# A four-layer model on one Trainium2 core: another order of heads, convolution inputs and taps, the sub-norm in four steps, and residual sums one chunk ahead

## The chip, the cores and the metric

The kernel runs on one core of a Trainium2 chip as one program. The metric is the device time of one execution in microseconds, taken from the hardware profiler. Five engines run their own instruction lists side by side and meet through semaphores: PE (matrix products), DVE (vector operations), ACT (activations), POOL (general work) and SP (which only issues the transfers of weights here). A wait at the head of an engine's list holds everything behind it.

## The reference, cut to what matters

512 tokens of width 1024 go through four layers and a last norm, in float32. Two of them end in a feed-forward network with a 3-tap convolution (up 1024 to 6144, gelu times value, down), the other two in one with a squared relu (width 4096).

```
# first_block: layer 0 attention, layer 1 a gated linear recurrence, each + conv_ffn
h = h + hybrid_attention_mixer(rms_norm(h), ...)   # 8 dilated heads, 4 differential heads:
    attn = p[:, :, 0] - lam * p[:, :, 1]
    ob   = rms_norm(attn @ vf, b_sub_norm) * (1 - lam_init)     # the "sub-norm"
h = h + recurrent_mixer(rms_norm(h), ...)          # uses softplus(-a_param)
# second_block: two hybrid layers
h  = rms_norm_2(x, g_mix);  split(h @ w_in) -> a_q a_k a_v b_qlat b_kvlat b_krope c_q c_k c_v c_f d_val d_gate
out_a = chunk_band_attention(a_q, a_k, a_v, rel_bias)
q  = rms_norm_2(b_qlat) @ w_uq ; kv = rms_norm_2(b_kvlat) @ w_ukv ; rotary on 32 of 96
out_b = block_causal_attention(q, k, v)            # latent heads
out_c = block_causal_attention(c_q, c_k, c_v, 1, cumsum(log_sigmoid(c_f)))   # forget heads
u = d_val * sigmoid(d_gate); u = conv31(u)         # 256 channels, 31 taps
out_d = silu(layer_norm(u))
x = x + sum_n(sigmoid(h @ w_gate + b_gate)[n] * (branches[n] @ w_branch[n])) @ w_o
x = x + square(relu(rms_norm_2(x) @ w_up)) @ w_down
```

## The kernel before, in words

The stream x is held transposed, as eight chunks of 128 channels by 512 tokens (`hT`). For exactness every product is three: operands are split into a high and a low part, and PE does high·high, high·low and low·high (L420, L421, L422 in `linear`; the same triple in L468 to L470, L541 to L543 and L770 to L772). One k-step is such a triple. The weights come as 470 slabs of 128 by 1024: SP loads one, ACT makes its high part (`w_hi`, L872), POOL the low part (`w_lo`, L1859). Three slabs are kept, so ACT's copy of slab n waits until PE has finished slab n-3.

The outputs of an activation layer are split in the same way: `take_high` (ACT, L923) and `take_low` (DVE, L1282), in that order; the pair is what PE reads next. `chunk` does it for the norm that begins a layer: ACT scales and squares a chunk (L896, L902), DVE makes its low part (L1297) and adds the squares (L1308); PE then sums over partitions and ACT and DVE make the root and its reciprocal (L917, L1323). Each product is scaled by that reciprocal on DVE afterwards (L1328). The residual sum of chunk o (L1316) adds the product's bank to `hT`.

PE writes eight banks of its accumulator memory. A bank may be written again when the reader named in `free` is done. In the hybrid layers the products go round three banks, 5, 6 and 7 (`next_bank`).

The order within a layer's attention is a list of steps written by `attention_steps`: for each block n the scores of block n, the softmax of n-1, then the extra steps that stand in `beside[n]`, then a step that is due from the sub-norm, then transposes and the mix of block n-2, then `behind[n]`. Every engine walks through the same list, each doing its part of each step. So an extra step placed early in the list stands ahead of the softmax of the next block on every engine. In the first layer the extra steps are the projections of pairs of heads (`qk`, with `qk_root`, `qk_norm`, and `qk_turn`, which transposes a pair on PE, L564), and products of the output projection (`out`, given as (output chunk, first k, last k), the sum of its parts k0 to k1 of the mixed heads y0 to y7). y4 to y7 are the differential heads with a sub-norm: `submean`, `subrec` (first half of the reciprocal, L1488), `subnorm` (second half L1491, the product L1493, and the two parts of y).

In a hybrid layer the extra steps are the latent heads' inputs (`latent`, `latent_parts`: reciprocal L1701, L1708, the split L1282), their keys, values and queries (`b_key` copied at L1720, `b_values`, `b_query`, rotated in L1663 to L1666), the forget heads' rows (`c_head`: a product of eight k-steps, and one DVE operation, L1656), the convolution's inputs (`d_input`: two products, and on DVE L1328, L1736 and L1740), 62 taps of the convolution (`tap`: even ones on DVE, L1795; odd ones a multiplication on ACT, L1225, and an addition on POOL, L1926), and the gated branches (`gated`: ten k-steps and four DVE operations). After the attention the convolution's layer norm (`conv_mean`, `conv_var`, `conv_norm`, `conv_out`) and more `gated` follow.

Of the kernel before, what the change touches and what calls it, by code (L numbers as in the profile page):

```python
# [119 lines left out]
def program(nc, x_in, small_in, fixed_in, heads_in, rel_in, pos_in, out):  # L120
# [3 lines left out]
    with ctx:  # L124
# [134 lines left out]
        def attention_steps(stage, units, beside, behind=None):  # L259
# [26 lines left out]
            for i, stage_ in enumerate(later):  # L286
                steps += beside.get(n_blocks + LAG + i, [])
                steps.append(stage_)
# [14 lines left out]
        pair_banks = [(5, 6), (7, 2)] + [((5, 6), (7, 5), (6, 7))[p % 3] for p in range(6)]  # L303
# [16 lines left out]
        parts0 = []  # L320
        for p, after in ((2, unit_steps(3)), (3, unit_steps(4)), (4, unit_steps(5)), (5, vb_steps(0))):
            parts0 += behind_next(p, after)
        parts0 += [[f] for f in unit_steps(6)] + behind_next(6, unit_steps(7))
        beside0 = {}
        for i, part in enumerate(parts0):
# [7 lines left out]
                  30: [(0, 5, 6), (1, 5, 6), (2, 5, 6)], 32: [(3, 0, 5)], 33: [(4, 0, 5)],  # L333
                  34: [(0, 6, 7), (1, 6, 7), (2, 6, 7), (3, 5, 7), (4, 5, 7)], 35: [(5, 0, 7)], 36: [(7, 0, 7)]}
# [4 lines left out]
        def qk_ready(n):  # L339
# [11 lines left out]
                   13: [("c_head", 5)], 14: [("c_head", 7)]}  # L351
# [6 lines left out]
        for i, f in enumerate(tap_list[:44]):  # L358
            behind2.setdefault(10 + i * 16 // 44, []).append(f)
# [503 lines left out]
        def scalar(A):  # L863
# [134 lines left out]
            for what, a in steps0:  # L998
# [32 lines left out]
                elif what == "subnorm":  # L1031
# [9 lines left out]


# [1080 lines left out]
```

## Time and profile before

| what | value |
|---|---|
| three runs, us | 2934.51, 2933.91, 2926.31 (median 2933.91) |
| the profiled execution, us | 2934.61, its span 2932.8, granted clock 0.982 |
| busy share | PE 96%, PE's weight loads 78%, DVE 46%, ACT 42%, POOL 42% |
| the chain that ended last | PE 85%, DVE 8%, ACT 3%, issue 2%, POOL 1% |

The profile names an instruction by its line. PE is busy nearly all the time, so what can be saved lies in PE's idle stretches, and in the stretches after them in which its clock is lower. The span is one execution; the profiled execution lies 0.7 us above the median.

### The profile page before, as it was taken

Reading aid. Unit: us, or ns where it says so; the run is one execution under the profiler, and the core shown is the slowest. Engines: PE = TensorE matmul, PEld = TensorE weight load, DVE = VectorE, ACT = ScalarE, POOL = GpSimd, SP = SyncE. Lnnn points to the kernel's source line nnn. Section 1 sums busy time; section 2 is a strip of 40 time slices with the busy share of each in tenths; the row PEclk is TensorE's granted clock in tenths of the full one; section 3 lists DMA queues with packets and bytes.
Section 4 is the critical chain, followed back from the end, with each engine's and each line's share of the span. In section 5 each row is a group of like instructions: output and inputs, shape, how many; then the busy total and the mean of one; then the engine's idle time right before and its main releaser. Section 6 shows DMA issues by size and latency. Waiting matters only on the chain.

```text
span 2932.8 us, 32425 instructions
## 1 busy us (share of the span) xinstructions
PE 2823.6 (96%) x12948; PEld 2281.5 (78%) x12948; DVE 1341.9 (46%) x2091; ACT 1223.7 (42%) x1793; POOL 1236.8 (42%) x550
## 2 busy tenths in 40 slices
PE   8998999999889999998999999999989999999998
PEld 7786788888667888876778788888767777888886
DVE  4565651545875415435656452022246565531113
ACT  3564442434544424334574434233235744342231
POOL 4222344444453444432446444444423464444442
PEclk9999999999989999998999999999999999999999
DMA  4211232232212323322222223232322222223232
GB/s 146 82 59 61 79 101 97 92 107 87 79 65 94 99 91 98 101 92 74 66 65 94 86 94 101 94 100 94 101 72 66 72 79 87 100 94 101 94 101 72
DMA packets 73926, 259.21 MB, mean 88 GB/s; under 512 B 9184, under 2 KB 9184, under 8 KB 73776
## 3 DMA queue, kind: packets, MB, share of 16 engines
q1 hardware_dynamic: 71680, 251.79, 26.8%
q10 hardware_dynamic: 2096, 5.36, 0.5%
q8 instruction: 102, 1.67, 0.2%
q14 instruction: 48, 0.39, 0.0%
HBM read 254.95 MB, written 2.13 MB: 88 GB/s over the span
## 4 chain that ended last, share of the span: by engine, by line
PE 85%; DVE 8%; ACT 3%; issue 2%; POOL 1%; DMA 0%; DVEq 0%; SPq 0%; ACTq 0%; POOLq 0%
PE ps L420 25%; PE ps L422 25%; PE ps L421 25%; PE ps L486 2%; PE ps L516 1%; PE ps L541 1%; PE ps L542 1%; PE ps L543 1%; POOL w_lo L1859 1%; PE ps L499 1%; PE ps L431 1%; PE ps L468 1%; PE ps L470 1%; PE ps L469 1%; ACT w_hi L872 1%
## 5 line engine op out<-in xcount | busy, mean ns | idle before, releaser
L1859 POOL TENSOR_TENSOR w_lo<-raw,w_hi 128x1024 fp32r<-128x1024 f32 x470 | 1135.6, 2419 | 1552.0 <-ACT w_hi L872 1551.6
L420 PE MATMUL ps<-xs,w_hi 128*128 128x512 f32 x2176 | 864.2, 397 | 17.8 <-POOL w_lo L1859 10.3
L421 PE MATMUL ps<-xs,w_hi 128*128 128x512 f32 x2176 | 849.3, 390 | 0.0
L422 PE MATMUL ps<-xs,w_lo 128*128 128x512 f32 x2176 | 849.0, 390 | 0.0
L872 ACT ACTIVATE w_hi<-raw 128x1024 fp32r<-128x1024 f32 x470 | 493.9, 1052 | 660.4 <-PE ps L422 615.4
L420 PE MATMUL ps<-hid,w_hi 128*128 128x512 f32 x1320 | 523.0, 396 | 43.7 <-DVE att L1736 18.1
L421 PE MATMUL ps<-hid,w_hi 128*128 128x512 f32 x1320 | 519.2, 393 | 0.0
L422 PE MATMUL ps<-hid,w_lo 128*128 128x512 f32 x1320 | 519.1, 393 | 0.0
L420 PEld LDWEIGHTS ps<-xs,w_hi 128*128 128x128 f32 x2176 | 409.7, 188 | 123.9 <-issue 15.0
L421 PEld LDWEIGHTS ps<-xs,w_hi 128*128 128x128 f32 x2176 | 410.0, 188 | 88.3 <-issue 4.8
L422 PEld LDWEIGHTS ps<-xs,w_lo 128*128 128x128 f32 x2176 | 409.8, 188 | 86.3
L420 PEld LDWEIGHTS ps<-hid,w_hi 128*128 128x128 f32 x1320 | 251.1, 190 | 103.9 <-DVE att L1736 19.0
L422 PEld LDWEIGHTS ps<-hid,w_lo 128*128 128x128 f32 x1320 | 251.1, 190 | 53.1
L421 PEld LDWEIGHTS ps<-hid,w_hi 128*128 128x128 f32 x1320 | 251.3, 190 | 52.0 <-issue 0.2
L1328 DVE TENSOR_TENSOR ps<-ps,rt 128x512 f32<-128x512 f32 x182 | 126.4, 697 | 267.6 <-PE ps L422 267.3
L1316 DVE TENSOR_TENSOR hT<-ps,hT 128x512 f32<-128x512 f32 x96 | 65.9, 687 | 337.7 <-PE ps L422 337.7
L1297 DVE SCALAR_TENSOR_TENSOR xs<-hT,small,xs 128x512 fp32r<-128x512 f32 x64 | 111.7, 1745 | 167.8 <-ACT xs L896 167.8
L1059 ACT ACTIVATE tmp<-ps,small 128x512 f32<-128x512 f32 x96 | 74.8, 779 | 219.4 <-DVE ps L1328 219.4
L1282 DVE TENSOR_TENSOR hid<-tmp,hid 128x512 fp32r<-128x512 f32 x120 | 85.6, 715 | 137.1 <-ACT hid L923 137.1
L930 ACT ACTIVATE pbuf<-pbuf,tiny 128x128 f32<-128x128 f32 (+3 forms) x160 | 88.7, 555 | 111.7 <-DVE tiny L1355 111.4
L1251 ACT ACTIVATE tmp<-tmp 128x512 f32<-128x512 f32 x64 | 40.4, 632 | 199.1 <-DVE tmp L1835 199.1
L923 ACT ACTIVATE hid<-tmp 128x512 fp32r<-128x512 f32 x128 | 80.5, 630 | 100.0 <-DVE tmp L1553 88.3
(212 smaller groups left out, 2651.8 us busy)
## 6 DMA issues: line engine op xcount, KB each, us to landing
raw<-in_weights SPq DMA_DIRECT2D x470, 512.0 KB, 3.5
hT<-in_x ACTq DMA_DIRECT2D x4, 512.0 KB, 9.6
btab<-in_rel SPq DMA_DIRECT2D x8, 256.0 KB, 3.7
out<-tmp ACTq DMA_DIRECT2D x8, 256.0 KB, 2.0
btab<-in_heads SPq DMA_DIRECT2D x6, 256.0 KB, 3.7
tmp<-in_heads SPq DMA_DIRECT2D x6, 256.0 KB, 4.4
common<-in_fixed ACTq DMA_DIRECT2D x1, 642.0 KB, 13.3
small<-in_small ACTq DMA_DIRECT2D x1, 368.5 KB, 5.0
```

Source lines behind the costliest of these rows:

```text
L420: pe.matmul(banks[bank][:], wh, rh, start=(k == 0), stop=False)
L421: pe.matmul(banks[bank][:], wh, rl, start=False, stop=False)
L422: last = pe.matmul(banks[bank][:], wl, rh, start=False, stop=(k == len(specs) - 1))
L872: ac.activation(w_hi[:, n % NPAIR, :], raw[:, n % NRAW, :], ACT.Copy).then_inc(*w_high.tick(n))
L923: ac.activation(dst, src, ACT.Copy).then_inc(*high.tick(event))
L930: ac.activation(pbuf[:, i % 6, 0:w], pbuf[:, i % 6, 0:w], ACT.Exp, bias=tcol(3 * i), scale=-1.0, accum_out=tcol(3 * i + 1)).then_inc(*rise ...
L1059: ac.activation(tmp[:, 4 + j % 6, :], banks[j % 6][:], ACT.Identity, bias=small[:, bc + ch:bc + ch + 1], scale=small[:, wc + 3 * ch + 2:wc ...
L1282: ve.tensor_tensor(pair[1], src, pair[0].bitcast(F32), ALU.subtract).then_inc(*low.tick(event))
L1297: ve.scalar_tensor_tensor(out=lo, in0=hT[:, c, :], scalar=col(gname, g0 + c), in1=hi.bitcast(F32), op0=ALU.mult, op1=ALU.subtract).then_in ...
L1316: ve.tensor_tensor(hT[:, o, :], banks[bank][:], hT[:, o, :], ALU.add).then_inc(*resid.tick(event, ("chunk", m, o)))
L1328: ve.tensor_tensor(banks[bank][:], banks[bank][:], rt[:], ALU.mult).then_inc(*scaled.tick(event))
L1859: gp.tensor_tensor(w_lo[:, n % NPAIR, :], raw[:, n % NRAW, :], w_hi[:, n % NPAIR, :].bitcast(F32), ALU.subtract).then_inc(*w_low.tick(n))
```

## The change

Seven parts. (1) A differential head's sub-norm has four steps instead of three: the split into high and low part is a step of its own, `sublow`, one block later, and the last output products are placed between the steps of the last heads. (2) The second bank of pair 3 (pairs count from 0) is 4 instead of 5, the other pairs keep theirs, and the transposition of pair 2 comes two products later. (3) The output products of y5 come at block 31 instead of 30, and those of outputs 3 and 4 are cut in two, so that y6's part comes last. (4) Hybrid layers: `c_head` 4 and 6 take the places of the convolution's first inputs at blocks 3 and 4, the convolution's inputs come at 7, 8, 10 and 11, and `b_query` 0 a block later. (5) The taps start at block 12 instead of 10, the last 18 stand four ahead of each of five gated steps instead of two ahead of each of nine, and the layer norm's steps come three gated steps sooner. (6) The softplus of the recurrence (19 small operations of DVE, one of ACT) goes from the end of layer 0's attention to the middle of its feed-forward network. (7) The residual sum of chunk o+1 is issued on DVE ahead of `chunk(o)`.

```diff
+            if later:
+                n = n_blocks + LAG
+                steps += later[:1] + beside[n] + later[1:2] + beside[n + 1] + later[2:] + beside[n + 2]
...
-            return [("submean", u), ("subrec", u), ("subnorm", u)] if stage == "first" and u >= 4 else []
+            return [("submean", u), ("subrec", u), ("subnorm", u), ("sublow", u)] if stage == "first" and u >= 4 else []
...
-        pair_banks = [(5, 6), (7, 2)] + [((5, 6), (7, 5), (6, 7))[p % 3] for p in range(6)]
+        pair_banks = [(5, 6), (7, 2), (5, 6), (7, 4)] + [((6, 7), (5, 6), (7, 5))[p % 3] for p in range(4)]
...
+        after = unit_steps(3)
+        parts0 = [[after[0], ("qk_root", 2), ("qk_norm", 2)], [after[1]], [after[2]], [after[3], ("qk_turn", 2)]]
+        for p, after in ((3, unit_steps(4)), (4, unit_steps(5)), (5, vb_steps(0))):
...
-                  30: [(0, 5, 6), (1, 5, 6), (2, 5, 6)], 32: [(3, 0, 5)], 33: [(4, 0, 5)],
-                  34: [(0, 6, 7), (1, 6, 7), (2, 6, 7), (3, 5, 7), (4, 5, 7)], 35: [(5, 0, 7)], 36: [(7, 0, 7)]}
+                  31: [(0, 5, 6), (1, 5, 6), (2, 5, 6)], 32: [(3, 0, 5)], 33: [(4, 0, 5)],
+                  34: [(3, 5, 6), (4, 5, 6)] + [(o, 6, 7) for o in range(5)], 35: [(5, 0, 7)], 36: [(7, 0, 7)]}
...
-                   3: [("latent_parts", 1), ("d_input", (0, 0))], 4: [("latent_parts", 0), ("d_input", (0, 1))],
-                   5: [("b_key", 0), ("b_key", 1), ("b_values", 0), ("b_query", 0)],
-                   6: [("b_query", 1), ("b_key", 2), ("b_key", 3)], 7: [("d_input", (1, 0))], 8: [("d_input", (1, 1))],
-                   9: [("b_query", 2), ("b_query", 3)], 10: [("c_head", 4)], 11: [("c_head", 6)], 12: [("gated", (0, 0))],
+                   3: [("latent_parts", 1), ("c_head", 4)], 4: [("c_head", 6), ("latent_parts", 0)],
+                   5: [("b_key", 0), ("b_key", 1), ("b_values", 0)],
+                   6: [("b_query", 0), ("b_query", 1), ("b_key", 2), ("b_key", 3)], 7: [("d_input", (0, 0))],
+                   8: [("d_input", (0, 1))], 9: [("b_query", 2), ("b_query", 3)], 10: [("d_input", (1, 0))],
+                   11: [("d_input", (1, 1))], 12: [("gated", (0, 0))], 13: [("c_head", 5)], 14: [("c_head", 7)]}
...
-            behind2.setdefault(10 + i * 16 // 44, []).append(f)
+            behind2.setdefault(12 + i * 14 // 44, []).append(f)
...
-        for i, (n, c) in enumerate([(1, c) for c in range(4, 8)] + [(2, c) for c in range(5)]):
-            steps2 += rest[2 * i:2 * i + 2] + [("gated", (n, c))]
-        steps2 += [("conv_mean", 0), ("gated", (2, 5)), ("conv_var", 0), ("gated", (2, 6)), ("conv_norm", 0), ("gated", (2, 7)),
-                   ("conv_out", 0)]
+        for i, g in enumerate([(1, c) for c in range(4, 8)] + [(2, 0)]):
+            steps2 += rest[4 * i:4 * i + 4] + [("gated", g)]
+        for c, what in enumerate(["conv_mean", "conv_var", "conv_norm", "conv_out"]):
+            steps2 += [("gated", (2, 1 + c)), (what, 0)]
+        steps2 += [("gated", (2, c)) for c in range(5, 8)]
...
-                elif what == "subnorm":
+                elif what == "sublow":
                     A.wait_ge(vec, ("subnorm", a))
                     take_high(y["first", a][0], tmp[:, 2, :], ("y", "first", a))
...
+                    if L == 0 and part == 0:
+                        softplus()
...
+            def residuals(at, group, m, name=None):
+
+                for o in range(8):
+                    event = (name or group) + (o,)
+                    V.wait_ge(product, group + (o,))
+                    if last_sum[o] is not None:
+                        V.wait_ge(resid, last_sum[o])
+                    ve.tensor_tensor(hT[:, o, :], banks[at[o]][:], hT[:, o, :], ALU.add).then_inc(
+                        *resid.tick(event, ("chunk", m, o)))
+                    last_sum[o] = event
+                    if m is not None and o:
+                        chunk(m, o - 1)
+                if m is not None:
+                    chunk(m, 7)
...
-                    take_low(y["first", a], b, ("y", "first", a))
-            for o in range(8):
-                residual(out_banks[o], o, ("attn", o), 1, ("attn_out", o))
-                chunk(1, o)
+                elif what == "sublow":
+                    take_low(y["first", a], tmp[:, 2, :], ("y", "first", a))
+            residuals(out_banks, ("attn_out",), 1, ("attn",))
```

ACT, the end of layer 0's attention, before: `L1029` is the root of the sub-norm of y6 and then y7, `L872` a weight's high part, `L923` the high part of y6 (first) and y7 (last), `L1024` the square of y7.

```order
L923 ACTIVATE hid<-tmp 128x512
L920 ACTIVATE pt<-ps 128x4x128
L1024 ACTIVATE tmp<-ps 128x512
L872 ACTIVATE w_hi<-raw 128x1024
L1029 ACTIVATE tmp<-ps,tiny 128x512
L872 ACTIVATE w_hi<-raw 128x1024 x2
L923 ACTIVATE hid<-tmp 128x512
```

And of the change (two lines lower there, so L874, L925, L1026 and L1031):

```order
L1026 ACTIVATE tmp<-ps 128x512
L925 ACTIVATE hid<-tmp 128x512
L874 ACTIVATE w_hi<-raw 128x1024
L1031 ACTIVATE tmp<-ps,tiny 128x512
L874 ACTIVATE w_hi<-raw 128x1024
L925 ACTIVATE hid<-tmp 128x512
L874 ACTIVATE w_hi<-raw 128x1024
```

The high part of y6 moved behind y7's square, and the high part of y7 from behind two weights' copies to between them.

DVE, the residual sums between the recurrence and its feed-forward network, before: `L1316` is a residual sum, `L1297` a chunk's low part, `L1308` the sum of squares.

```order
L1316 TENSOR_TENSOR hT<-ps,hT 128x512
L1297 SCALAR_TENSOR_TENSOR xs<-hT,small,xs 128x512
L1316 TENSOR_TENSOR hT<-ps,hT 128x512
L1297 SCALAR_TENSOR_TENSOR xs<-hT,small,xs 128x512
L1308 TENSOR_TENSOR tmp<-tmp 128x512
L1316 TENSOR_TENSOR hT<-ps,hT 128x512
L1297 SCALAR_TENSOR_TENSOR xs<-hT,small,xs 128x512
```

And of the change, where these are L1323, L1302 and L1313:

```order
L1323 TENSOR_TENSOR hT<-ps,hT 128x512 x2
L1302 SCALAR_TENSOR_TENSOR xs<-hT,small,xs 128x512
L1323 TENSOR_TENSOR hT<-ps,hT 128x512
L1302 SCALAR_TENSOR_TENSOR xs<-hT,small,xs 128x512
L1313 TENSOR_TENSOR tmp<-tmp 128x512
L1323 TENSOR_TENSOR hT<-ps,hT 128x512
```

Each residual sum stands one chunk earlier: the first two are issued together, and what follows a residual sum is the chunk before it.

DVE, a hybrid layer between the softmax of block 3 (`L1377`, first row) and the copy of key 0, before: `L1701` to `L1282` is `latent_parts` 0, `L1328`, `L1736`, `L1740` the convolution's input, `L1766` a memset for the forget heads, `L1355` to `L1377` the softmax of block 5, `L1720` the copy.

```order
L1377 TENSOR_SCALAR pbuf<-pbuf,tiny 128x512
L1701 RECIPROCAL tmp<-tmp 128x512
L1703 TENSOR_SCALAR tiny<-small 128x2
L1708 SCALAR_TENSOR_TENSOR att<-att,tiny,tmp 128x512
L1282 TENSOR_TENSOR hid<-att,hid 128x512
L1708 SCALAR_TENSOR_TENSOR att<-att,tiny,tmp 128x512
L1282 TENSOR_TENSOR hid<-att,hid 128x512
L1328 TENSOR_TENSOR ps<-ps,rt 128x512
L1736 SCALAR_TENSOR_TENSOR att<-tmp,ps 128x512
L1740 SCALAR_TENSOR_TENSOR att<-att,rt 128x512
L1766 MEMSET aug 128x1024
```

And of the change (L1710 to L1287 is `latent_parts` 0, L1665 `c_head` 6, L1729 the copy):

```order
L1389 TENSOR_SCALAR pbuf<-pbuf,tiny 128x512
L1665 SCALAR_TENSOR_TENSOR att<-ps,rt 128x512
L1710 RECIPROCAL tmp<-tmp 128x512
L1712 TENSOR_SCALAR tiny<-small 128x2
L1717 SCALAR_TENSOR_TENSOR att<-att,tiny,tmp 128x512
L1287 TENSOR_TENSOR hid<-att,hid 128x512
L1717 SCALAR_TENSOR_TENSOR att<-att,tiny,tmp 128x512
L1287 TENSOR_TENSOR hid<-att,hid 128x512
L1775 MEMSET aug 128x1024
```

The convolution's three operations are gone from between `latent_parts` 0 and the memset, and the operation of `c_head` 6 stands ahead of the reciprocal; that of `c_head` 4 stands ten rows higher, behind `latent_parts` 1.

## Rows read from the trace of the kernel before

**Rows 1.** the page's first part: busy us, share of the span, instructions, by engine

```profile
PE 2823.6 (96%) x12948; PEld 2281.5 (78%) x12948; DVE 1341.9 (46%) x2091; ACT 1223.7 (42%) x1793; POOL 1236.8 (42%) x550
```

**Rows 2.** PE's waits by line and releaser: us in all, times, longest

```profile
PE ps L420 <- DVE att L1736: 18.1, 2, 9.1
```

**Rows 3.** timeline of PE: start, us, instruction [idle before <-releaser]

```profile
84.52 2.14 PE L564 MATMUL ps<-common,tmp 128*128 128x128 f32 x8 [4.24 <-DVE tmp L1435]
240.75 0.79 PE L420 MATMUL ps<-hid,w_hi 128*128 128x512 f32 x1 [3.20 <-DVE hid L1282]
280.18 0.50 PE L420 MATMUL ps<-hid,w_hi 128*128 128x512 f32 x1 [3.49 <-DVE hid L1282]
300.72 0.50 PE L420 MATMUL ps<-xs,w_hi 128*128 128x512 f32 x1 [1.55 <-DVE xs L1297]
319.93 0.50 PE L420 MATMUL ps<-xs,w_hi 128*128 128x512 f32 x1 [1.33 <-POOL w_lo L1859]
326.28 0.50 PE L420 MATMUL ps<-xs,w_hi 128*128 128x512 f32 x1 [0.59 <-POOL w_lo L1859]
882.14 0.50 PE L420 MATMUL ps<-xs,w_hi 128*128 128x512 f32 x1 [1.10 <-DVE xs L1297]
884.88 0.67 PE L420 MATMUL ps<-xs,w_hi 128*128 128x512 f32 x1 [1.76 <-DVE xs L1297]
1377.27 0.79 PE L420 MATMUL ps<-hid,w_hi 128*128 128x512 f32 x1 [9.07 <-DVE att L1736]
1654.14 0.50 PE L420 MATMUL ps<-hid,w_hi 128*128 128x512 f32 x1 [0.88 <-DVE hid L1282]
```

**Rows 4.** stretches: us, PE busy (instructions), granted clock, DMA share, GB/s

```profile
84.00:90.00 6.00, 5.49 (x23) 0.52 0.28 90
240.00:248.00 8.00, 7.25 (x18) 0.58 0.10 21
280.00:286.00 6.00, 5.82 (x18) 0.72 0.22 87
300.00:304.00 4.00, 2.95 (x9) 1.00 0.48 131
884.00:890.00 6.00, 5.12 (x13) 0.72 0.14 40
1369.00:1387.00 18.00, 8.32 (x29) 0.53 0.14 50
```

**Rows 5.** timeline of DVE and ACT, end of layer 0's attention

```profile
271.28 0.75 DVE L1493 SCALAR_TENSOR_TENSOR tmp<-ps,tiny,tmp 128x512 f32<-128x512 f32 x1
276.11 1.06 ACT L872 ACTIVATE w_hi<-raw 128x1024 fp32r<-128x1024 f32 x1 [4.38 <-PE ps L422]
277.07 0.61 ACT L923 ACTIVATE hid<-tmp 128x512 fp32r<-128x512 f32 x1
```

**Rows 6.** timeline of DVE, start of the two convolution networks

```profile
307.29 3.57 DVE L1512 SCALAR_TENSOR_TENSOR spb<-spb 128x8 f32<-128x8 f32 x7
311.52 3.35 DVE L1323 RECIPROCAL rt<-tmp 128x512 f32<-128x512 f32 x1
884.07 0.75 DVE L1297 SCALAR_TENSOR_TENSOR xs<-hT,small,xs 128x512 fp32r<-128x512 f32 x1 [0.79 <-ACT xs L896]
```

**Rows 7.** timeline of DVE, hybrid layer 0, blocks 4 and 5

```profile
1375.18 0.69 DVE L1328 TENSOR_TENSOR ps<-ps,rt 128x512 f32<-128x512 f32 x1
1377.25 1.21 DVE L1740 SCALAR_TENSOR_TENSOR att<-att,rt 128x512 f32<-128x512 f32 x1
1380.87 0.68 DVE L1720 COPY att<-ps 64x512 f32<-64x512 f32 x1
```

**Rows 8.** a stretch of gated steps: busy us of PE, PEld, DVE, ACT, POOL

```profile
1560.00:1622.00 62.00, 62.00 (x276) 51.14 (x275) 38.08 (x35) 23.08 (x30) 39.64 (x20) 1.00 0.27 86
```

**Rows 9.** groups in that stretch: busy us, mean ns | idle before <-releaser

```profile
L1795 DVE SCALAR_TENSOR_TENSOR att<-att,small 128x490 f32<-128x490 f32 (+8 forms) x9 | 15.5, 1724 | 0.0
L1926 POOL TENSOR_TENSOR att<-att 128x490 f32<-128x490 f32 (+8 forms) x9 | 12.1, 1346 | 10.6 <-ACT att L1225 10.6
```

More of the change, by code:

```diff
@@ L285, in attention_steps @@
                 later += ends_of(stage, late)
-            for i, stage_ in enumerate(later):
-                steps += beside.get(n_blocks + LAG + i, [])
-                steps.append(stage_)
+            if later:
+                n = n_blocks + LAG
+                steps += later[:1] + beside[n] + later[1:2] + beside[n + 1] + later[2:] + beside[n + 2]
             return steps
         def ends_of(stage, u):
-            return [("submean", u), ("subrec", u), ("subnorm", u)] if stage == "first" and u >= 4 else []
+            return [("submean", u), ("subrec", u), ("subnorm", u), ("sublow", u)] if stage == "first" and u >= 4 else []
         def is_lam(stage, u):
@@ L1040, in scalar, with softplus @@
             square_chunk(1, 7)
-            A.wait_ge(vec, "softplus_in")
-            ac.activation(s2, s2, ACT.Exp, scale=-1.0).then_inc(*act.tick("softplus"))
+            def softplus():
+                A.wait_ge(vec, "softplus_in")
+                ac.activation(s2, s2, ACT.Exp, scale=-1.0).then_inc(*act.tick("softplus"))
             def network(L, m):
@@ L1309, in chunk @@
                         *summed.tick((m, c)))
-            def residual(bank, o, event, m, before, emit=True):
-                V.wait_ge(product, before)
-                if last_sum[o] is not None:
-                    V.wait_ge(resid, last_sum[o])
-                ve.tensor_tensor(hT[:, o, :], banks[bank][:], hT[:, o, :], ALU.add).then_inc(*resid.tick(event, ("chunk", m, o)))
-                last_sum[o] = event
+            def residuals(at, group, m, name=None):
[11 more added lines that the diff above has]
+                    chunk(m, 7)
             last_sum = [None] * 8
@@ L1515, in log1p_exp_neg, with softplus @@
                 V.wait_ge(step)
[L1518 to L1530 removed]
+            def softplus():
+                ap0 = lay["rec_a_param"][0]
+                apar = small[:, ap0:ap0 + 8]
+                chain(ve.tensor_scalar(s1, apar, -1.0, None, ALU.mult))
+                V.wait_ge(step)
+                ve.tensor_tensor(s2, apar, s1, ALU.max).then_inc(*vec.tick("softplus_in"))
+                V.wait_ge(act, "softplus")
+                log1p_exp_neg(sp8, s2, s3, s4)
+                chain(ve.scalar_tensor_tensor(out=sp8, in0=s1, scalar=0.0, in1=sp8, op0=ALU.max, op1=ALU.add))
+                V.wait_ge(step)
+                ga0, gx0 = lay["rec_gate_a_b"][0], lay["rec_gate_x_b"][0]
+                ve.tensor_scalar(sp8, sp8, 2.0, None, ALU.mult)
+                ve.tensor_scalar(hb[:, 0:8], small[:, ga0:ga0 + 8], 0.5, None, ALU.mult)
+                ve.tensor_scalar(hb[:, 8:16], small[:, gx0:gx0 + 8], 0.5, None, ALU.mult).then_inc(*vec.tick("softplus"))
             def network(L, m):
@@ L1554, in network @@
                         take_low(hi_lo(hid, c % 12), g, ("hid", L, c))
-                    for o in range(8):
-                        residual((0, 1, 2, 3)[o % 4], o, ("down", L, part, o), m + 1 if part else -1, ("down", L, part, o))
-                        if part:
-                            chunk(m + 1, o)
+                    if L == 0 and part == 0:
+                        softplus()
+                    residuals((0, 1, 2, 3) * 2, ("down", L, part), m + 1 if part else None)
             network(0, 1)
@@ L1617, in vector @@
                     rec_0(c)
-            for o in range(8):
-                residual(rec_banks[o], o, ("rec", o), 3, ("rec_out", o))
-                chunk(3, o)
+            residuals(rec_banks, ("rec_out",), 3, ("rec",))
             network(1, 3)
@@ L1822, in hybrid @@
                 m = 5 + 2 * L
-                for o in range(8):
-                    residual((0, 1, 2, 3)[o % 4], o, ("w_o", L, o), m, ("w_o", L, o))
-                    chunk(m, o)
+                residuals((0, 1, 2, 3) * 2, ("w_o", L), m)
                 for part in range(2):
@@ L1838, in hybrid @@
                         take_low(hi_lo(hid, c % 16), b, ("hid2", L, c))
-                    for o in range(8):
-                        residual((0, 1, 2, 3)[o % 4], o, ("down2", L, part, o), m + 1 if part else -1, ("down2", L, part, o))
-                        if part:
-                            chunk(m + 1, o)
+                    residuals((0, 1, 2, 3) * 2, ("down2", L, part), m + 1 if part else None)
             for L in range(2):
```

16 lines of the change are left out of this document (removed).

## The prediction

> **What bounds the kernel now.** I read the page's first part, then PE's waits grouped by releaser, then PE's own timeline for the place of each wait, then the granted clock around these places, then DVE and ACT just before them. The first part says that PE is busy 2823.6 us [rows 1]; the span is 2932.8, so all of PE's idle time is 109 us, and no edit here removes a product. Whatever this change gives has to come from idle stretches of PE, or from the stretches behind them in which PE works at its lower clock. The grouped waits show the largest single cause: the convolution's input on DVE, 18.1 us in two waits, one per hybrid layer [rows 2]. The timeline gives the others [rows 3]; in each row the number in brackets is how long PE stood idle and which instruction ended it. The stretches show the second price [rows 4]: behind the idles of 3 us and more the granted clock averages 0.52 to 0.72, its lower level (1.2 GHz of 2.4) for part of the stretch. What that costs beside the idle is PE's busy time times what is missing to 1.00: 2.6 us at 84 to 90, 3.0 at 240 to 248, 1.6 at 280 to 286, 1.4 at 884 to 890, 3.9 at 1369 to 1387. The stretch 300 to 304 holds an idle of 1.55 and stayed at 1.00, so an idle that shrinks to about 1.5 can give its clock back too; but 1.76 at 884.88 did not stay at 1.00, so 1.5 to 2 is the edge.
>
> **The change part by part**, in the order of the program, all in us, plus is time gained.
>
> Pair 2 (84.52). PE waits 4.24 there for the normed pair on DVE, and loses 2.6 in the clock: 6.8 at stake [rows 3, 4]. With the transposition two products later PE goes on with the next score and the products of pair 3. The third score then waits instead: it needs the softmax of the second, which on DVE stands behind the same normed pair. I put that new wait at about 2. So 2.2 of idle are sure, and some clock: I take 3.0, bounds 1.5 and 6.8. The changed bank of pair 3 only takes away one wait for a copy, inside these bounds.
>
> y5 (240.75). PE waits 3.20 for y5's low part, and loses 3.0 in the clock [rows 3, 4]. The products of y5 now come a block later, so PE meets the next mix first. That mix writes bank 4, which the sub-norm's product frees only about 1.5 before y5's low part is done, so a wait of about 1.7 stays: 1.5 gained. Whether the clock returns is open, since 1.7 is at the edge named above. I take 3.8; bounds 1.5 and 6.2.
>
> y6. Its high part now stands on ACT behind y7's square, and its low part behind that: at most one high (0.61 [rows 5]) and one low (0.7, as the operations of this shape in [rows 7]) later than PE wants it. I take -0.9; bounds -1.3 and 0.
>
> y7 (280.18). The sub-norm's product ended at 271.28 + 0.75 = 272.03, but the high part waited on ACT behind a weight's high part, which itself waited 4.38 for PE and started at 276.11 [rows 5]. In the change the high part stands ahead of that copy: high 0.61, low 0.7, done at about 273.5, and PE reached the place at 280.18 - 3.49 = 276.69. So the 3.49 and the clock's 1.6 go: +5.1; bounds 3.5 and 5.1. Behind it the weight's copy is 0.6 later, and PE needs that slab only after the products it still has.
>
> Into network 0 (300 to 326). Two effects. A chunk's circle on DVE and ACT no longer holds the wait for the residual sum of the next: of 1.55 and the two waits of 0.3 after it I take 1.2. And the softplus leaves DVE: seven of its operations take 3.57, and only behind them could the root's reciprocal start, at 311.52 [rows 6]. It starts some 3 earlier, everything after it too, and the waits of 1.33 and 0.59 for weights at 319.93 and 326.28, which follow from slabs freed late, should go: 1.9. Together 3.1; bounds 1.2 (the late weights have their own cause) and 3.8. In its new place the softplus lies in front of the down product of network 0, whose first bank is wanted again only after four sums of twelve k-steps: hidden, cost 0. If that cover failed it would cost what it takes, some 6.
>
> Into network 1 (882 and 884.88). The last two chunks of the recurrence's sum: 1.10 + 1.76 + 1.4 of clock [rows 3, 4]. The circle of a chunk was sum, high, low, add; now a sum stands ahead of the low part (0.75 [rows 6]) and the wait of 0.79 in front of it is filled. DVE's own time per chunk, 0.7 + 0.75 + 0.7 = 2.15, is then the circle, instead of 882.14 to 884.88 = 2.74. Over seven chunks this is more than the wait, so nearly all goes: +4.2; bounds 2.0 and 4.3. The other places where `residuals` stands show no wait in PE's timeline; there the last chunk's low part comes one sum later, which the k-steps in hand hide. At the start of hybrid layer 0 the position angles stand behind one sum more: -0.7, bounds -0.7 and 0.
>
> Hybrid layers (1377.27). The idle of 9.07 [rows 3] is the wait of key 1 for a bank that holds a convolution input. In the change the banks of keys and values come from `c_head`, which DVE leaves early, so keys 0 and 1 and the first half of the values start at once. But the second half of the values takes the bank of key 0, and that copy (1380.87 [rows 7]) still stands behind `latent_parts` 0 on DVE, which is busy without a gap. What goes from in front of it is 1375.18 to 1377.25 + 1.21, that is 3.28 [rows 7]; what comes is two `c_head` operations of 0.69 each. So the copy is done 1.9 earlier, and PE stops one step later in its list for nearly as long. Because query 0 now follows the next score, key 3 meets query 0's rotation, up to 0.7. I take +1.2 a layer, 2.4 in all; bounds 0 and 3.8. The stall itself does not go.
>
> Taps and layer norm. `conv_out` stands three gated steps before the next layer's use of it, so the 0.88 at 1654.14 [rows 3] goes in both layers: 1.8, bounds 0 and 1.8. Four taps a gated step instead of two I cost at 0: in the stretch of gated steps PE has no idle, DVE works 38.1 and POOL 39.6 of 62 [rows 8], which is the cover; what fails if it does not hold is the third rival.
>
> Sum: 3.0 + 3.8 - 0.9 + 5.1 + 3.1 + 4.2 - 0.7 + 2.4 + 1.8 = 21.8. Against the profiled execution, 2934.61, that is 2912.8; against the median of the runs, 2933.91, it is 2912.1. I say 2912. The lower bounds add up to 1.5 + 1.5 - 1.3 + 3.5 + 1.2 + 2.0 - 0.7 = 7.7, the upper ones to 31.8; the likeliest case's own range is 2903 to 2927.
>
> **The rivals.**
>
> First, the stall named after the convolution's input dissolves wholly, as its name in the grouped waits suggests. Then each layer gives 9.07 + 3.9 instead of 1.2, 11.8 more, twice: 2912 - 24 = 2888. For it: the row names that instruction and no other. Against it: DVE's list, in which the copy that PE needs next stands behind the whole of `latent_parts` 0.
>
> Second, idle moves but does not go: PE, freed at one wait, runs into the next producer. Then only the gains with a shown margin stay, y7's idle 3.49, the recurrence's 1.10 + 1.76 and `conv_out`'s 1.8, less 0.9 and 0.7: 6.6, so 2927. For it: the pair, y5 and the hybrid stall do just this by my own working. Against it: at 276.69 and at 884 nothing else is late.
>
> Third, on the slower side: the denser taps. The five gated steps in each hybrid layer that carry four taps have one more on DVE (mean 1.72) and one more on POOL (mean 1.35) than the stretch I read [rows 9]. If the two engines do not overlap there, each added pair stands in PE's way: 5 x 2 x (1.72 + 1.35) = 30.7, and 2912 + 31 = 2943. It decides from the point at which POOL's and DVE's time in nine gated steps, 39.6 + 12.1 and 38.1 + 15.5, can no longer run side by side in 62; each alone fits. For it: the taps on DVE are stretched where POOL works, the mean is 1.72 against 0.7 for other operations of nearly the same size [rows 7, 9]. Against it: in the stretch read PE never waited, and the steps after the five carry no taps. The Trainium skill, page "SBUF — State Buffer", section "SBUF: two separate sides", says that a DVE operation with two inputs in SBUF and a GpSimd operation take turns at a shared port, each holding it for its whole length; by that rule the taps of both engines add up instead of lying side by side, and the time would go the third rival's way. The stretched mean agrees with the rule; no row tells how much slack is left.
>
> **How the numbers follow.** A measurement of this kernel can tell about 0.3%, 8.8 us, from no change, so faster means below 2925.1. The forecast case has 0.70 and lies nearly wholly below that (0.68). The first rival has 0.05, faster. The second has 0.15, its centre near the border: half faster, half within 0.3%. The third has 0.07, slower. That the parts do not act as I read them, and the time stays where it was, has 0.03. Faster 0.68 + 0.05 + 0.07 = 0.80; within 0.3% 0.02 + 0.08 + 0.03 = 0.13; slower 0.07. The range 2898 to 2929 leaves out the first and third rivals and little else.
>
> **What would show it.** In the changed kernel's timeline of PE: no idle before the products of y7, about 1.7 in place of 3.20 at y5, about 2 in place of 4.24 at the third score, none above 0.5 in the last chunks into network 1, a first idle of some 7 to 8 in each hybrid layer that names the copy of key 0, none at `conv_out`. In the stretch with four taps a step PE busy without a gap; an idle there that names `gated`'s DVE operations would be the third rival. The forecast is wrong if the hybrid stall is under 3 (the first rival) or if new idles of more than 1 appear where PE had none.

## The result and the profile after

On one chip the changed kernel took 2911.72 us (median of four runs, 2908.06 to 2912.05) beside 2930.11 for the kernel before (four runs, 2925.98 to 2934.51). The ratio is 0.9927, 95% interval 0.9913 to 0.9941: 0.73% faster, some 21 us. The medians lie 18.4 apart; the fourth run of the kernel before, 2925.98, moved its median from 2933.91 to 2930.11. The forecast was 2912.

The first part of the page of the changed kernel (busy us, share of the span, instructions), against [rows 1]:

```profile
PE 2809.8 (97%) x12948; PEld 2274.4 (78%) x12948; DVE 1278.3 (44%) x2091; ACT 1223.1 (42%) x1793; POOL 1239.4 (43%) x550
```

PE is busy 14 us less with the same instructions, which agrees with the mean granted clock, 0.988 against 0.982; the span fell by 26.5, so idle went down by 12.7. These two profiled executions are a slow one of before (2934.61) and the fastest of the change (2908.06), so they lie 26.5 apart where the runs as a whole lie about 21 apart; what can make the difference stands in the last section.

PE's waits by line and releaser (us in all, times, longest), against [rows 2]:

```profile
PE ps L772 <- DVE att L1729: 17.2, 2, 9.4
...
PE ps L518 <- ACT pt L922: 4.7, 3, 2.0
...
PE ps L422 <- DVE xs L1302: 1.6, 1, 1.6
PE ps L422 <- DVE hid L1287: 0.8, 2, 0.6
```

In the kernel before the same two places, the copy of key 0 (L1720 there) and a copy of transposed weights on ACT (L920 there), were:

```profile
PE ps L770 <- DVE att L1720: 2.8, 2, 1.4
PE ps L516 <- ACT pt L920: 1.2, 3, 0.7
```

The wait that carried the name of the convolution's input (18.1) is gone from the list, and one of nearly the same size stands under another name, the copy of key 0: the two names together were 20.9 and are 17.2. The second line above, which grew from 1.2 to 4.7, is the part that the forecast did not have.

PE's timeline in the changed kernel at the places of [rows 3] (start, us, instruction, idle before and its releaser):

```profile
85.76 1.25 PE L488 MATMUL ps<-att 64*128 64x384 f32 x4 [1.55 <-DVE tiny L1367]
234.13 2.42 PE L518 MATMUL ps<-pt,att 128*128 128x512 f32 x8 [1.78 <-DVE tmp L1505]
253.65 0.50 PE L422 MATMUL ps<-hid,w_hi 128*128 128x512 f32 x1 [0.56 <-DVE hid L1287]
286.41 0.50 PE L422 MATMUL ps<-xs,w_hi 128*128 128x512 f32 x1 [1.56 <-DVE xs L1302]
1353.33 0.58 PE L772 MATMUL ps<-w_hi,hid 128*128 128x256 f32 x1 [9.39 <-DVE att L1729]
1530.18 3.54 PE L518 MATMUL ps<-pt,att 128*64 128x512 f32 x7 [2.00 <-ACT pt L922]
2173.66 0.58 PE L772 MATMUL ps<-w_hi,hid 128*128 128x256 f32 x1 [7.85 <-DVE att L1729]
```

And the stretches that answer to [rows 4] (us, PE busy, granted clock, DMA share, GB/s):

```profile
84.00:92.00 8.00, 6.45 (x36) 0.79 0.19 66
232.00:240.00 8.00, 6.22 (x25) 1.00 0.20 66
268.00:276.00 8.00, 8.00 (x37) 1.00 0.23 74
860.00:880.00 20.00, 20.00 (x88) 1.00 0.18 55
1344.00:1358.00 14.00, 4.67 (x20) 0.63 0.17 46
1529.00:1537.00 8.00, 6.71 (x24) 0.79 0.18 62
```

4.24 at the pair became 1.55 at the third score; 3.20 at y5 became 1.78 at the next mix, with the clock at 1.00 instead of 0.58; y6 is late by 0.56; at y7 nothing is left, and nothing in the last chunks into network 1. In the hybrid layers 9.07 became 9.39 and 7.85, ended by the copy of key 0. At the last attention block of a hybrid layer a wait of 2.00 stands where 0.25 was, with a granted clock of 0.79 behind it.

### The profile page after: what moved, and what is told of

Its sections match the earlier page's. It is cut to its first block, busy times and chain, and to the rows that moved or that the text cites. A ratio compares the mean times of both kernels' runs of the same rounds, so it can differ in the third digit from the quotient of the medians.

```text
span 2906.3 us, 32429 instructions
## 1 busy us (share of the span) xinstructions
PE 2809.8 (97%) x12948; PEld 2274.4 (78%) x12948; DVE 1278.3 (44%) x2091; ACT 1223.1 (42%) x1793; POOL 1239.4 (43%) x550
## 4 chain that ended last, share of the span: by engine, by line
PE 87%; DVE 7%; ACT 2%; issue 2%; POOL 1%; DMA 0%; DVEq 0%; SPq 0%; ACTq 0%
PE ps L422 26%; PE ps L424 25%; PE ps L423 25%; PE ps L488 2%; PE ps L518 2%; PE ps L543 1%; PE ps L545 1%; PE ps L544 1%; PE ps L501 1%; PE ps L433 1%; DVE tmp L1605 1%; PE ps L470 1%; PE ps L471 1%; PE ps L472 1%; POOL w_lo L1863 1%
## 5 line engine op out<-in xcount | busy, mean ns | idle before, releaser
L874 ACT ACTIVATE w_hi<-raw 128x1024 fp32r<-128x1024 f32 x470 | 493.6, 1052 | 646.7 <-PE ps L424 601.3
L1323 DVE TENSOR_TENSOR hT<-ps,hT 128x512 f32<-128x512 f32 x96 | 66.2, 691 | 569.3 <-PE ps L424 569.3
L1340 DVE TENSOR_TENSOR ps<-ps,rt 128x512 f32<-128x512 f32 x182 | 126.5, 698 | 272.7 <-PE ps L424 272.3
L1287 DVE TENSOR_TENSOR hid<-tmp,hid 128x512 fp32r<-128x512 f32 x120 | 87.0, 726 | 136.1 <-ACT hid L925 136.0
L925 ACT ACTIVATE hid<-tmp 128x512 fp32r<-128x512 f32 x128 | 80.5, 631 | 90.7 <-DVE tmp L1565 87.2
L1842 DVE SCALAR_TENSOR_TENSOR tmp<-ps,rt 128x512 f32<-128x512 f32 x64 | 44.3, 692 | 158.1 <-PE ps L424 157.9
```

What stands on the lines that cost most here:

```text
L874: ac.activation(w_hi[:, n % NPAIR, :], raw[:, n % NRAW, :], ACT.Copy).then_inc(*w_high.tick(n))
L925: ac.activation(dst, src, ACT.Copy).then_inc(*high.tick(event))
L1287: ve.tensor_tensor(pair[1], src, pair[0].bitcast(F32), ALU.subtract).then_inc(*low.tick(event))
L1323: ve.tensor_tensor(hT[:, o, :], banks[at[o]][:], hT[:, o, :], ALU.add).then_inc(*resid.tick(event, ("chunk", m, o)))
L1340: ve.tensor_tensor(banks[bank][:], banks[bank][:], rt[:], ALU.mult).then_inc(*scaled.tick(event))
```

## The experiments

Two numbers are given for each: the ratio of its runs to those of the kernel before on the same chip, and stretches of its profile between the same instructions of PE. The ratios are good to about 0.13%, some 4 us, so the stretches carry the verdicts on single terms. A stretch comes from one execution of each kernel, and where one is named with two values it was taken against two of them.

**Only the residual sums.** The kernel before with this edit alone (and its like in the five places):

```diff
-            for o in range(8):
-                residual(rec_banks[o], o, ("rec", o), 3, ("rec_out", o))
-                chunk(3, o)
+            residuals(rec_banks, ("rec_out",), 3, ("rec",))
```

> The kernel before with the residual sums one chunk ahead and nothing else. My reading (DVE's circle per chunk was the limit, 2.74 us, and is 2.15 now): the waits of 1.10 and 1.76 into network 1 and the clock behind them go, 4 to 5, and of the 1.55 and 0.32 into network 0 little goes, 0 to 1; with that about 5 us less than before (ratio 0.998). The rival (PE freed here runs into the next late producer): 0 to 1 us less, and a wait of about 1 stands somewhere in the first products of network 1.

Ratio 0.9965, interval 0.9953 to 0.9978. The last wait of the recurrence and the first of hybrid layer 0, in this run:

```profile
855.70 0.50 PE L420 MATMUL ps<-hid,w_hi 128*128 128x512 f32 x1 [3.49 <-POOL hid L1878]
1278.24 0.50 PE L468 MATMUL ps<-w_hi,xs 128*128 128x512 f32 x1 [2.18 <-POOL w_lo L1854]
```

The stretch between them is 422.54; in the kernel before it is 859.11 to 1287.28, 428.17, and in the run below, which has the old sums, 427.50. So 5.0 to 5.6 come from here, and no wait takes its place. Into network 0, from the wait of 1.55 to that of 7.2 for a weight, it is 463.72 against 465.17: 1.45. My reading holds in its places: 6.4 to 7.1 in all, more than the 5 expected. The ratio says some 10 us (its interval 6.5 to 13.8), so the runs gain more than these two stretches show; what the rest is stays open.

**Only the hybrid layers** (order, taps, layer norm; the two tables and two loops of the diff):

> The kernel before with the hybrid layers' new order and the denser taps, and nothing else. By the prediction: 4 us less (1.2 a layer at the keys, 0.9 a layer at conv_out). By the trace of the changed kernel: a wait of 2.0 for a copy of transposed weights at the last block of the attention, with 2 to 2.5 of lower clock behind it, in both layers, eats that: within 2 us of before. By the rival that the stall at the keys dissolves: 24 us less.

Ratio 0.9999, interval 0.9990 to 1.0008: no change. Three waits of this run:

```profile
1374.99 0.58 PE L771 MATMUL ps<-w_hi,hid 128*128 128x256 f32 x1 [9.39 <-DVE att L1721]
1552.29 1.07 PE L517 MATMUL ps<-pt,att 128*64 128x512 f32 x2 [2.00 <-ACT pt L921]
2373.84 1.07 PE L517 MATMUL ps<-pt,att 128*64 128x512 f32 x2 [2.01 <-ACT pt L921]
```

The prediction's 4 us are not there, and the second expectation, made from the trace of the changed kernel, is what came: the keys' wait renamed, and two waits of 2.00 where 0.25 was.

**Only layer 0's attention** (sub-norm, bank, transposition, output products):

> The kernel before with the changes in layer 0's attention (sub-norm in four steps, pair 3's bank, the transposition of pair 2, the output products) and nothing else. By the prediction's terms: 3.0 + 3.8 - 0.9 + 5.1 = 11 us less; by the trace of the changed kernel up to the first chunk of network 0: 14 less. By the rival that idle only moves: y7's 3.5 less 0.9, about 3 us less.

Ratio 0.9943, interval 0.9930 to 0.9955. Its waits are those of the changed kernel:

```profile
85.86 1.40 PE L487 MATMUL ps<-att 64*128 64x384 f32 x4 [1.71 <-DVE tiny L1356]
234.33 2.42 PE L517 MATMUL ps<-pt,att 128*128 128x512 f32 x8 [1.78 <-DVE tmp L1494]
253.85 0.50 PE L421 MATMUL ps<-hid,w_hi 128*128 128x512 f32 x1 [0.56 <-DVE hid L1283]
286.63 0.50 PE L421 MATMUL ps<-xs,w_hi 128*128 128x512 f32 x1 [1.55 <-DVE xs L1298]
```

The last row stands at 286.63 from the start; in the three profiles with the old attention the same instruction with the same wait of 1.55 stands at 297.35 (hybrid layers alone), 296.91 (sums alone) and 300.72 (the kernel before). That is 10.3 to 14.1; the prediction's terms give 11.0, and the rival that idle only moves gave 3. The three have the same attention, so the 3.8 between them are not the change's. The ratio says some 17 us (its interval 13 to 20.5), above the 11 and the 14 expected. The rival is ruled out either way; the size is known only to several us.

**The softplus back in its old place**, in the changed kernel (the diff shows DVE; ACT has the same two edits):

```diff
+            softplus()
+
             def network(L, m):
...
-                    if L == 0 and part == 0:
-                        softplus()
```

> The changed kernel with the softplus back in its old place, between the attention and the network of layer 0. If the late reciprocal caused the waits for weights at the start of network 0 (1.33 and 0.59): they come back, and the time is about 2 us above the changed kernel, ratio to before 0.993 to 0.994. If the weights were late of their own: the same time as the changed kernel.

Ratio 0.9919, interval 0.9905 to 0.9932, median 2910.41. The waits for weights are back:

```profile
304.00 0.50 PE L422 MATMUL ps<-xs,w_hi 128*128 128x512 f32 x1 [1.02 <-POOL w_lo L1863]
310.34 0.50 PE L422 MATMUL ps<-xs,w_hi 128*128 128x512 f32 x1 [0.60 <-POOL w_lo L1863]
```

From the wait of 1.55 at 286 to that of 7.18 it takes 749.96 - 286.26 = 463.70, in the changed kernel 747.91 - 286.41 = 461.50. The stretch is 2.2 longer, as expected. The time is not: the ratio should have been 0.993 to 0.994, and it is no higher than the changed kernel's 0.9927 above and 0.9921 below.

**The changed kernel once more**, beside the next two:

> The changed kernel once more, so that the next three and the softplus run stand beside it on one chip with more runs. Ratio to before 0.992 to 0.994. If the softplus is worth its stage (2.2 us between the first chunk of network 0 and the recurrence), this run's median lies about 2 us below that of the run with the softplus in its old place; if only the clock's luck differs, within 1.

Ratio 0.9921, interval 0.9908 to 0.9933, median 2908.94. That is 1.5 below the run with the old softplus, between the two expectations, but on another chip, where the kernel before is 2.8 lower too (2931.29 against 2934.09); the ratios, 0.9921 and 0.9919, show no difference. The runs of one kernel spread over 6 us (2905.84 to 2911.66), so the softplus is shown by its stretch alone.

**Fewer taps in the attention's blocks:**

```diff
-        for i, f in enumerate(tap_list[:44]):
-            behind2.setdefault(12 + i * 14 // 44, []).append(f)
+        for i, f in enumerate(tap_list[:38]):
+            behind2.setdefault(12 + i * 14 // 38, []).append(f)
...
-        for i, g in enumerate([(1, c) for c in range(4, 8)] + [(2, 0)]):
+        for i, g in enumerate([(1, c) for c in range(4, 8)] + [(2, 0), (2, 1)]):
...
```

> The changed kernel with 38 instead of 44 taps in blocks 12 to 25 of the hybrid layers, and 24 instead of 18 behind them (four ahead of each of six gated steps). My theory: the wait of 2.0 at the last attention block is there because two taps of DVE, 3.8 us beside POOL, stand ahead of the scaling that ACT's tanh and then ACT's copy of the transposed weights wait for. Then it falls below 0.6 in both layers, its lower clock goes too, and the time is 4 to 8 us below the changed kernel (ratio to before 0.990 to 0.991). Rival: the wait comes from the order of the gated steps, not the taps: no change (0.993). If four taps a gated step were too many, an idle of PE shows between gated steps.

Ratio 0.9897, interval 0.9882 to 0.9911, against 0.9921 for the changed kernel beside it: 7 us by the ratios, though the intervals just overlap. The waits at the last block, which were 2.00 and 2.03 for the copy on ACT:

```profile
1530.68 2.37 PE L518 MATMUL ps<-pt,att 128*64 128x512 f32 x14 [0.74 <-DVE pt L1396]
2346.72 2.37 PE L518 MATMUL ps<-pt,att 128*64 128x512 f32 x14 [0.75 <-DVE pt L1396]
```

No idle shows between gated steps, with four taps each. From the latent heads' score that waits 0.98 to the start of the next layer's first rows this run takes 1385.37 to 2097.12, 711.75; the changed kernel 714.38; the kernel before 1413.30 to 2126.24, 712.94. The longest wait is 0.74 and 0.75, for a copy on DVE, not below 0.6 as expected; that for the copy on ACT is 0.25 again, as in the kernel before, and the clock behind them stays. So the price was paid in the blocks, not in the gated steps behind them, and fewer taps in the blocks are enough to end it.

**Keys and values ahead of `latent_parts` 0**, in the changed kernel:

```diff
-                   3: [("latent_parts", 1), ("c_head", 4)], 4: [("c_head", 6), ("latent_parts", 0)],
-                   5: [("b_key", 0), ("b_key", 1), ("b_values", 0)],
+                   3: [("latent_parts", 1), ("c_head", 4)], 4: [("c_head", 6), ("b_key", 0), ("b_key", 1), ("b_values", 0), ("latent_parts", 0)],
+                   5: [("c_head", 5)],
...
-                   11: [("d_input", (1, 1))], 12: [("gated", (0, 0))], 13: [("c_head", 5)], 14: [("c_head", 7)]}
+                   11: [("d_input", (1, 1))], 12: [("gated", (0, 0))], 13: [("gated", (0, 1))], 14: [("c_head", 7)]}
...
```

> The changed kernel with keys 0 and 1 and the values of the latent heads ahead of latent_parts 0, the forget heads' row product 5 between them and query 0, and one gated step earlier in its place. My theory: the idle of 9.4 and 7.9 is DVE's list (key 0's copy behind latent_parts 0), not a lack of work. Then it is gone or below 2, a wait of 2 to 3 comes at key 3, and the time is 12 to 18 us below the changed kernel (ratio 0.987 to 0.989). Rival: the idle moves whole to the next step that needs DVE (query 0 or key 3): within 4 us of the changed kernel (0.992 to 0.993).

Ratio 0.9872, interval 0.9855 to 0.9890, median 2895.32: 14 us below the changed kernel beside it, as expected. Two waits of layer 0:

```profile
1344.34 0.38 PE L772 MATMUL ps<-w_hi,hid 128*128 128x256 f32 x1 [1.76 <-DVE att L1665]
1364.08 0.80 PE L422 MATMUL ps<-hid,w_hi 128*128 128x512 f32 x1 [4.22 <-DVE att L1675]
```

In the place of 9.39 stands 1.76, and key 3 waits 4.2, more than the 2 to 3 expected, for the rotation of query 0. Both hybrid layers, from the first product of values to the final root, take 1262.78 to 2881.80, 1619.0, against 1630.3 in the changed kernel. Not all of this is the keys: the wait of 2.00 at the last block is 0.48 here, with the same 44 taps. DVE's wait for the tanh of an earlier gated step in the changed kernel, and in this run that same wait, the last block's two taps, and PE behind them:

```profile
1514.38 0.69 DVE L1682 TENSOR_TENSOR tmp<-tmp,ps 128x512 f32<-128x512 f32 x1 [2.46 <-ACT tmp L1152]
```

```profile
1519.11 0.69 DVE L1682 TENSOR_TENSOR tmp<-tmp,ps 128x512 f32<-128x512 f32 x1 [1.09 <-ACT tmp L1152]
1529.07 3.85 DVE L1804 SCALAR_TENSOR_TENSOR att<-att,small 128x493 f32<-128x493 f32 x2
1534.79 1.07 PE L518 MATMUL ps<-pt,att 128*64 128x512 f32 x2 [0.48 <-ACT pt L922]
```

The taps take 3.85 again, but PE finishes its products 5.2 after they start (1534.31 against 1529.07) instead of 3.7 (1528.18 against 1524.47 in the changed kernel, whose rows stand in the next section). DVE comes to them some 1.5 earlier beside PE, and most of that is the shorter wait at L1682. So the thick taps cost only where PE is close behind.

**Both edits together**, the keys' order and 38 taps:

> Both of the last two edits together. If they act in different places, as I think, their gains add: 16 to 24 us below the changed kernel, ratio to before 0.985 to 0.988.

Ratio 0.9878, interval 0.9864 to 0.9893, median 2897.86: no better than the keys alone. The ratio is at the edge of the expected band, but the sum that I expected did not come: 11 by the medians and 13 by the ratios below the changed kernel, instead of 16 to 24. The two edits do not act in different places, as I had thought: with the keys alone the wait of 2.00 was 0.48 already. By the profile both hybrid layers take 1615.0, 4 less than with the keys alone, and no wait of over 0.3 is left at the last blocks; 1.6 of the 4 is the clock at their start (see the last section).

**Keys 2 and 3 ahead of queries 0 and 1**, in the kernel with both edits:

```diff
-                   6: [("b_query", 0), ("b_query", 1), ("b_key", 2), ("b_key", 3)], 7: [("d_input", (0, 0))],
+                   6: [("b_key", 2), ("b_key", 3), ("b_query", 0), ("b_query", 1)], 7: [("d_input", (0, 0))],
```

> The kernel with both edits (keys earlier, 38 taps), and keys 2 and 3 ahead of queries 0 and 1. My theory: the idle of 4.2 is key 3 waiting for the bank of query 0, whose rotation on DVE (three operations, one stretched to 2.5) stands behind the softmax of block 6. Keys 2 and 3 then go at once, query 1 waits about 2 for key 2's copy instead: 2 to 3 us a layer, 4 to 7 in all below the run of both edits beside it. Rival: what is saved comes back as a wait of the scores of the latent heads for the rotations: within 2 us of it.

Ratio 0.9846, interval 0.9832 to 0.9861, median 2885.17. One row of its timeline, and the stretch around it (us, PE busy, granted clock, DMA share, GB/s):

```profile
1357.60 0.47 PE L422 MATMUL ps<-hid,w_hi 128*128 128x512 f32 x1 [1.64 <-DVE att L1729]
```

```profile
1334.00:1366.00 32.00, 26.92 (x131) 1.00 0.26 83
```

4.2 is 1.64, and the clock stays at 1.00 through the stretch that stood at 0.53 in the kernel before. This is the best of the versions tried: 47 us below the kernel before by the medians, and 22 to 24 below the change by the ratios (0.9846 against 0.9921 and 0.9927).

**Both edits once more**, beside it:

> Both edits together once more. By the stretches of the profiles the hybrid layers take 9 us less than in the changed kernel with thinner taps alone and 4 less than with the keys alone; so the median should be 2 to 5 us below that of the keys alone (2895.3), ratio to before 0.985 to 0.987. If it is again 0.988, the taps' gain does not add to the keys' in time, whatever one profile shows.

Ratio 0.9870, interval 0.9853 to 0.9887, median 2892.38. The median is 3 below the keys alone (on another chip), in the expected band; the ratio is at its edge, and the intervals of the three runs overlap. The 9 us less than with the thinner taps alone, from which I expected it, was misread: between the same instructions it is 6.9 (1621.97 against 1615.03). So a gain of the taps beyond the keys is not settled; by what is left of the wait (0.48 and 0.49 with the keys alone) it can't be much. The version with keys 2 and 3 first is 7.2 below this run, just above the 4 to 7 expected.

## Why the prediction was right, and where it was not

The time came out within 1 us of the forecast, by terms of which most were right and two were off in opposite directions. That it came so near is luck: the gain is known to some 4 us only, and the forecast was taken from a median of the kernel before that one more run moved by 3.8. The table sets the terms beside the stretches, between the same instructions of PE, of the runs that hold one part alone; plus is time gained.

| term | forecast | measured | from |
|---|---|---|---|
| layer 0's attention: pair, y5, y6, y7 | +11.0 | +10.3 to +14.1 | attention alone against the three profiles with the old one, start to first chunk |
| sums, into network 0 | +1.2 | +1.45 | sums alone |
| softplus | +1.9 | +2.2 | softplus put back |
| sums, into network 1 | +4.2 | +5.0 to 5.6 | sums alone |
| start of hybrid layer 0 | -0.7 | not told apart | the clock differs there between runs |
| hybrid layers: keys, layer norm, taps | +4.2 | -2.2 to -0.7 | hybrid alone, 1632.6, against 1630.5, 1631.7 and 1632.0 with the old order; the changed kernel's 1630.3 has a faster clock at its start, worth 1.6 |
| sum | 21.8 | 16.8 to 22.7 | ratio of the whole: 0.73%, some 21 |

The ratios of the parts (0.9965, 0.9999, 0.9943) multiply to 0.9907, some 27 us, with an uncertainty of some 6 by their intervals; the whole is 21 with 4, so they do not contradict it.

The steps in layer 0's attention were right in kind one by one. Between the two profiles PE's mix of y5 is 5.89 earlier (222.27 to 216.38): the pair, for which I took 3.0 of the 6.8 at stake. PE's mix of y7 is 9.76 earlier (259.05 to 249.29): 3.9 for y5's products, for which I took 3.8, with the 1.7 that stays measured as 1.78. The sum for y7's sub-norm is 8.92 earlier (266.10 to 257.18), 0.84 less: y6, for which I took -0.9. The chunk that waits 1.55 is 14.31 earlier (300.72 to 286.41): 5.4 for y7, for which I took 5.1. Between the run of the attention alone and that of the hybrid layers alone the same four are 3.6, 2.7, -0.85 and 5.3. So y6 and y7 hold to 0.3, and the pair and y5, where the clock is in play, to 1 to 3.

The prediction's edge for the clock, an idle of 1.5 to 2, does not hold. In the kernel before itself a granted clock of 1.00 follows an idle of 2.15 (851.24), and one of 0.72 an idle of 0.88 (2126.24). The two stretches (us, PE busy, granted clock, DMA share, GB/s):

```profile
851.00:857.00 6.00, 4.38 (x18) 1.00 0.25 85
2126.00:2132.00 6.00, 5.76 (x22) 0.72 0.00 0
```

So the clock of 1.00 behind the 1.78 at y5 could not be counted on: behind the same wait in the run with the softplus put back (1.79) it is 0.79 over 232 to 240.

The step that failed is "Four taps a gated step instead of two I cost at 0". I looked for the price in the five gated steps behind the attention, and there it is 0, as said: no idle between them. But the same edit also put 44 taps into 14 blocks instead of 16, and the price is there. These rows of the changed kernel, DVE, ACT and POOL at the last block, show it (start, us, engine, instruction, idle before and its releaser):

```profile
1524.47 3.84 DVE L1804 SCALAR_TENSOR_TENSOR att<-att,small 128x493 f32<-128x493 f32 x2
1528.23 0.69 DVE L1340 TENSOR_TENSOR ps<-ps,rt 128x512 f32<-128x512 f32 x1
...
1528.95 0.69 ACT L1152 ACTIVATE tmp<-ps,small 128x512 f32<-128x512 f32 x1 [4.39 <-DVE ps L1340]
1529.54 0.59 ACT L922 ACTIVATE pt<-ps 128x512 f32<-128x512 f32 x1
...
1523.69 1.31 POOL L1930 TENSOR_TENSOR att<-att 128x493 f32<-128x493 f32 x1 [2.67 <-ACT att L1230]
1524.96 2.83 POOL L1863 TENSOR_TENSOR w_lo<-raw,w_hi 128x1024 fp32r<-128x1024 f32 x1
```

Two taps of DVE, 3.84 us, stand ahead of the scaling of a gated step (L1340); it starts when they end, ACT's tanh (L1152) waits for it, and behind the tanh, in ACT's list, stands the copy of transposed weights (L922) that PE waits 2.00 for at 1530.18. Where the last block has one tap of DVE less, PE waits 0.25 for that copy. From the latent heads' last wait to the next layer's start the change takes 1.4 more in layer 0 (714.38 against 712.94), where I had 0.9 less, and 2.0 more in layer 1 (686.93 against 684.90): 2.3 and 2.9 for a term that I set at 0, where the thinner taps give back 2.6 and 3.2. PE's idle in this part of layer 0 is nearly the same, 3.14 before and 3.23 after, as `conv_out`'s 0.88 went; the loss is the clock behind the 2.00, which is 0.79 over 1529 to 1537: 6.71 x 0.21 = 1.4. A sign that the prediction itself had named for being wrong, a new idle of more than 1, did appear here. My third rival had the right mechanism, DVE and POOL in each other's way, at the wrong place, and its price of 31 was far too high: both layers together fell some 5 short.

The first of the two taps begins beside POOL's addition (1523.69 to 1525.00), and the second ends 0.5 after POOL's low part of a weight (1524.96 to 1527.79). The shortest tap takes 0.71 in either kernel, so 2.4 of the 3.84 is waiting. The Trainium skill, "SBUF — State Buffer", section "SBUF: two separate sides", has this as a rule: a DVE operation with two inputs in SBUF and one of GpSimd take turns at a shared port, each for its whole length. The rows agree, and the prediction, which weighed that rule for the five gated steps, should have asked it of the blocks too.

The keys were as worked out in kind: the name of the wait changed, and its size by little. Of the 1.2 a layer forecast, the stretches show more in layer 0 and the same or nothing in layer 1. From the first product of values to the latent heads' score that waits 0.98, the hybrid run takes 124.22 in layer 0 (1282.83 to 1407.05) and the attention run, with the old order, 126.00 (1274.46 to 1400.46): 1.8. In layer 1 it is 106.89, against 106.62 in the attention run, 107.86 in the kernel before and 108.22 in the run of the sums. One reading of the prediction was wrong: DVE is not "busy without a gap" in front of the copy; in the kernel before it stood 0.70, 0.69 and 0.66 for ACT there (ahead of 1372.52, 1374.57 and 1376.53). The first rival, that the stall dissolves, was wrong for this order; the run with keys and values in front of `latent_parts` 0 shows an order in which most of it does.

## What to carry to other kernels

A wait's name in a grouped list tells which instruction came last, not what stands behind it in the same engine's list; before an edit that removes the named one, walk that list on to the next thing that is waited for. When an edit spreads work anew, price each place that becomes denser, not only the one that the edit is about. To move a stall in kernels with lists in order, move the short copies that free a bank ahead of the long chain, and put a product without inputs from that chain between.

## What was not expected of the hardware

The granted clock after the same idle is not the same in each execution. Code and idle are the same at 106 in the kernel before and in the run of the hybrid layers alone (1.63 and 1.62 for ACT), and at 1262 in the changed kernel and in the run with the keys moved (2.18 and 2.17); the stretches behind (us, PE busy, granted clock, DMA share, GB/s) are, in this order of kernels:

```profile
106.00:112.00 6.00, 5.04 (x30) 0.72 0.11 43
```

```profile
106.00:112.00 6.00, 5.71 (x45) 1.00 0.02 6
```

```profile
1262.00:1269.00 7.00, 6.23 (x27) 1.00 0.55 154
```

```profile
1262.00:1269.00 7.00, 6.22 (x20) 0.76 0.47 156
```

Once it fell and once it stayed, at each place, worth about 1.5 each time (PE's busy time times what is missing to 1.00). What decides it is not shown. With a dozen idles of 1 to 3 us in a program, that is enough for the spread between runs of one kernel (2925.63 to 2935.88 for the kernel before over all these runs), and it can be why two single profiles differ by 26.5 where the kernels differ by 21; no run separates it from other causes. It agrees with this that the best version, with keys 2 and 3 first, has the mean clock 0.994 against 0.982: a shorter idle can be worth more than its length.
